# A new order for the fill of a chunked recurrence, and one scaling moved from VectorE to GpSimd

## The reference

```python
def step(S, inp):
    r_t, w_t, k_t, v_t, a_t, b_t = inp
    sa = jnp.einsum('bhij,bhj->bhi', S, a_t)
    S = (S * w_t[:, :, None, :] + sa[..., None] * b_t[:, :, None, :]
         + v_t[..., None] * k_t[:, :, None, :])
    return S, jnp.einsum('bhij,bhj->bhi', S, r_t)
_, y = lax.scan(step, S0, seq_in)   # over 528 positions
```

## Time and profile before

| | |
|---|---|
| median of 3 runs | 1512.23 us (1511.02 to 1512.6) |
| time of the profiled execution | 1514.68 us |
| its span in the profile | 1513.0 us |
| TensorE busy | 1436.7 us, 95% of the span |
| VectorE busy | 1033.1 us, 68% |
| ScalarE busy | 739.6 us, 49% |
| GpSimd busy | 93.5 us, 6% |
| chunk stage | from 878.15 us to about 1069 us of the span |

### The profile page before, as it was taken

The page is one execution under the profiler, slowest core; times in us unless marked ns, Lnnn a source line. Parts: engine busy times, 40 slices in busy tenths (PEclk is TensorE's granted clock), DMA queues, the critical chain, the costliest instruction groups (busy, mean ns, idle before and its releaser), DMA issues.

```text
span 1513.0 us, 30344 instructions
## 1 busy us (share of the span) xinstructions
PE 1436.7 (95%) x12931; PEld 1322.3 (87%) x12931; DVE 1033.1 (68%) x1463; ACT 739.6 (49%) x1071; POOL 93.5 (6%) x120
## 2 busy tenths in 40 slices
PE   6999999999999999998999967999799999999997
PEld 5898898999999999998999756889467898899986
DVE  5667577588844787577868665776678884488732
ACT  4555465445532455457588532433454553255422
POOL 3010011000030000000000231110000000000010
PEclk9999999999999999999999977999999999999999
DMA  4212221423433333555222232332333343334331
GB/s 126 67 57 63 64 70 50 113 84 98 123 92 100 92 92 88 158 162 173 83 74 77 70 85 47 60 57 40 113 84 98 98 123 104 95 85 112 86 96 56
DMA packets 283990, 136.78 MB, mean 90 GB/s; under 512 B 65449, under 2 KB 278593, under 8 KB 283601
## 3 DMA queue, kind: packets, MB, share of 16 engines
q1 hardware_dynamic: 283552, 134.77, 32.4%
q10 hardware_dynamic: 304, 0.08, 0.0%
HBM read 124.33 MB, written 10.49 MB: 89 GB/s over the span
## 4 chain that ended last, share of the span: by engine, by line
PE 74%; DVE 11%; ACT 6%; issue 3%; DMA 3%; POOL 1%; SPq 0%; DVEq 0%; POOLq 0%; ACTq 0%
PE psg L1882 25%; PE psx L1723 13%; PE psg L1723 11%; PE psg L2688 6%; PE psg L590 2%; DVE w_lo L136 2%; PE psx L590 2%; PE psg L618 2%; PE psg L674 1%; ACT rest_hi L330 1%; PE psx L3334 1%; DVE rest_lo L429 1%; DVE sum_lo L446 1%; ACT rest L316 1%; ACT w_hi L132 1%
## 5 line engine op out<-in xcount | busy, mean ns | idle before, releaser
L132 ACT ACTIVATE w_hi<-w_raw 128x1024 fp32r<-128x1024 f32 (+1 forms) x122 | 141.9, 1164 | 209.8 <-PE psg L1882 148.1
L1882 PE MATMUL psg<-mid_hi_l,w_hi 128*128 128x264 f32 (+1 forms) x720 | 232.8, 323 | 2.3 <-DVE w_lo L136 1.3
L1882 PE MATMUL psg<-mid_lo_l,w_hi 128*128 128x264 f32 (+1 forms) x720 | 231.6, 322 | 0.0
L1882 PE MATMUL psg<-mid_hi_l,w_lo 128*128 128x264 f32 (+1 forms) x720 | 231.0, 321 | 0.0
L136 DVE TENSOR_TENSOR w_lo<-w_raw,w_hi 128x1024 fp32r<-128x1024 f32 (+1 forms) x121 | 165.0, 1365 | 77.5 <-ACT w_hi L132 77.0
L1882 PEld LDWEIGHTS psg<-mid_hi_l,w_hi 128*128 128x128 f32 x720 | 135.3, 188 | 14.1 <-DVE w_lo L136 2.0
L1882 PEld LDWEIGHTS psg<-mid_lo_l,w_hi 128*128 128x128 f32 x720 | 135.3, 188 | 10.5 <-issue 0.2
L1882 PEld LDWEIGHTS psg<-mid_hi_l,w_lo 128*128 128x128 f32 x720 | 135.4, 188 | 10.3
L2688 PE MATMUL psg<-x_hi,w_hi 128*128 128x264 f32 (+1 forms) x320 | 99.7, 312 | 7.9 <-DVE w_lo L136 7.9
L2688 PE MATMUL psg<-x_lo,w_hi 128*128 128x264 f32 (+1 forms) x320 | 98.8, 309 | 0.0
L2688 PE MATMUL psg<-x_hi,w_lo 128*128 128x264 f32 (+1 forms) x320 | 98.7, 309 | 0.0
(11 more groups left out here) (518 smaller groups left out, 4336.1 us busy)
## 6 DMA issues: line engine op xcount, KB each, us to landing
w_raw<-in_w_ffn_out_dram SPq DMA_DIRECT2D x40, 704.0 KB, 4.7
w_raw<-in_w_qkv_dram SPq DMA_DIRECT2D x24, 512.0 KB, 3.7
w_raw<-in_w_rkv_dram SPq DMA_DIRECT2D x24, 512.0 KB, 3.9
x_raw_l<-in_w_ffn_in_dram SPq DMA_DIRECT2D x18, 512.0 KB, 4.1
x_raw_l<-in_w_ffn_in_dram SPq DMA_DIRECT2D x36, 256.0 KB, 4.7
w_raw<-in_w_ffn_in_dram SPq DMA_DIRECT2D x16, 512.0 KB, 3.8
y_raw_l<-in_w_ffn_in_dram SPq DMA_DIRECT2D x16, 512.0 KB, 4.0
y_raw_l<-in_w_ffn_in_dram SPq DMA_DIRECT2D x32, 256.0 KB, 4.5
```

Of the source, the lines that this page charges most:

```text
L132: k.nc.scalar.activation(k.w_hi[j][:, 0:kt, :], k.raw[j][:, 0:kt, :], ACT.Copy).then_inc(k.hi_ready[j].h, 1)
L1882: done = k.nc.tensor.matmul(self.bank(i, c), w[:, t, :], x, start=t == 0 and n == 0, stop=t == count - 1 and n == 2)
```

## The change

Five things change in `chunk_stage`.

1. The fill is written out as a list of its own on each engine, and the loop of steps starts at 0. TensorE turns and multiplies chunk 0 (`turn_bk`, `turn_v`, `quads`, `a_v`) before `l_products(2)`; VectorE does the two `keys` of chunk 0 before `small_blocks(0)`; in step 0 the gate, a filler and the state come earlier than before.
2. `turn_v` writes the lower 64 partitions instead of the upper, and calls `transpose` instead of a product with the identity. To match, the two planes of `bk` and the two halves of `uv` and `akm` change places.
3. `low_kept` becomes two buffers.
4. SyncE's order becomes, for each n, `keep_inverse(n)`, `fetch_inverse(n)`, then `keep_low(n+1)`, `fetch_lanes(n+1)`. In the fill `keep_low(0)`, `keep_low(1)` and their lanes go first.
5. The scaling of `rr` moves from VectorE's `products` to GpSimd's, as its third operation, ahead of the signal `scaled_p`.

```diff
             def keep_low(n):
                 sp.wait_ge(low_r.h, n + 1)
-                if n:
-                    sp.wait_ge(lane_in.h, 16 * n)
+                if n >= 2:
+                    sp.wait_ge(lane_in.h, 16 * (n - 1))
                 for half in range(2):
-                    sp.dma_start(by_heads(k.low_kept, half), low[n % 3][half_rows(half), :, :]).then_inc(low_out.h, 16)
+                    sp.dma_start(by_heads(k.low_kept[n % 2], half), low[n % 3][half_rows(half), :, :]).then_inc(low_out.h, 16)
...
-            for c in range(-3, CHUNKS - 2):
-                if c + 3 < CHUNKS:
-                    keep_low(c + 3)
-                    fetch_lanes(c + 3)
-                if c == -3:
...
-                else:
-                    keep_inverse(c + 2)
-                    fetch_inverse(c + 2)
+            fetch_lanes(0)
+            keep_low(1)
+            fetch_lanes(1)
...
+            for n in range(CHUNKS):
+                keep_inverse(n)
+                fetch_inverse(n)
+                if 1 <= n < CHUNKS - 1:
+                    keep_low(n + 1)
+                    fetch_lanes(n + 1)
...
         def gpsimd(pool):
...
-                nc.gpsimd.tensor_tensor(bk[n % 3][:, :, 0, :], chunk(r.aa, n), ch.w_inv[:], ALU.mult)
-                nc.gpsimd.tensor_tensor(chunk(r.kk_in, n), chunk(r.kk_in, n), ch.w_inv[:], ALU.mult).then_inc(scaled_p.h, 1)
...
+                nc.gpsimd.tensor_tensor(bk[n % 3][:, :, 1, :], chunk(r.aa, n), ch.w_inv[:], ALU.mult)
+                nc.gpsimd.tensor_tensor(chunk(r.kk_in, n), chunk(r.kk_in, n), ch.w_inv[:], ALU.mult)
+                nc.gpsimd.tensor_tensor(chunk(r.rr, n), chunk(r.rr, n), ch.w_ext[:, :, 1:C + 1], ALU.mult).then_inc(scaled_p.h, 1)
...
         def vector(dve):
             def products(n):
                 dve.wait_ge(exps.h, n + 1)
-                nc.vector.tensor_tensor(chunk(r.xn, n), chunk(r.xn, n), ch.w_ext[:, :, 0:C], ALU.mult)
-                nc.vector.tensor_tensor(chunk(r.rr, n), chunk(r.rr, n), ch.w_ext[:, :, 1:C + 1], ALU.mult)\
+                nc.vector.tensor_tensor(chunk(r.xn, n), chunk(r.xn, n), ch.w_ext[:, :, 0:C], ALU.mult)\
                     .then_inc(scaled_v.h, 1)
...
             products(1)
-            dve.wait_ge(scaled_v.h, 2)
+            keys(0, 0)
+            keys(0, 1)
+            small_blocks(0)
+            last_blocks(0)
+            products(2)
+            small_blocks(1)
+            last_blocks(1)
+            products(3)
+            small_blocks(2)
             steps(dve, step)
...
                 pe.wait_ge(bkt_r.h, n + 1)
                 settle()
                 for m in range(KT):
-                    last = mm(pair_ps[C:P, m // 4, (m % 4) * P:(m % 4) * P + P], r.vv[:, m, n * C:n * C + C], k.ident[:],
-                              start=True, stop=True)
+                    last = nc.tensor.transpose(pair_ps[0:C, m // 4, (m % 4) * P:(m % 4) * P + P],
+                                               r.vv[:, m, n * C:n * C + C], k.ident[:])
                 last.then_inc(tv_d.h, 1)
...
             pe.wait_ge(k.pads.h, 16)
             front_evicted(pe)
+            l_products(0)
+            turn_bk(0)
+            keep(8)
+            l_products(1)
+            turn_v(0)
+            keep(8)
+            quads(0, 0)
+            keep(8)
+            quads(0, 1)
+            keep(8)
+            a_v(0, 0)
+            keep(32)
+            l_products(2)
+            keep(24)
             steps(pe, step)
```

More of the change, by code:

```diff
@@ L2967, in steps @@
         def steps(eng, step):
-            for c in range(-3, CHUNKS):
-                step(c, c + 1, c % 2, 0 <= c, 0 <= c + 1 < CHUNKS)
+            for c in range(CHUNKS):
+                step(c, c + 1, c % 2, c + 1 < CHUNKS)
         res_in, g_in, g_split, gate_d, gate_r = (
@@ L3046, in decays, with lower @@
                 if n > 1:
-                    nc.scalar.activation(bk[(n - 1) % 3][:, :, 1, :], chunk(r.kk_in, n - 1), ACT.Copy).then_inc(bk_r.h, 1)
+                    nc.scalar.activation(bk[(n - 1) % 3][:, :, 0, :], chunk(r.kk_in, n - 1), ACT.Copy).then_inc(bk_r.h, 1)
                 nc.scalar.activation(ch.w_ext[:, :, 1:C + 1], chunk(r.gs, n), ACT.Exp, scale=DECAY)
                 nc.scalar.activation(ch.w_inv[:], chunk(r.gs, n), ACT.Exp, scale=-DECAY).then_inc(exps.h, 1)
-            def step(c, n, q, chain, prep):
+            def lower(n):
+                act.wait_ge(lps.h, n + 1)
+                nc.scalar.activation(low[n % 3][:], l_ps, ACT.Copy).then_inc(low_r.h, 1)
@@ L3052, in step @@
+            def step(c, n, q, prep):
                 p = 1 - q
-                if c + 3 < CHUNKS:
-                    act.wait_ge(lps.h, c + 4)
-                    nc.scalar.activation(low[c % 3][:], l_ps, ACT.Copy).then_inc(low_r.h, 1)
+                if c + 3 < CHUNKS and c:
+                    lower(c + 3)
                 if prep:
-                    act.wait_ge(tb_d.h, n + 1)
-                    nc.scalar.activation(bkt[p][:].rearrange("p m a c -> p (m a) c"),
-                                         pair_ps.rearrange("p b (m c) -> p (b m) c", c=C),
-                                         ACT.Copy).then_inc(bkt_r.h, 1)
@@ L3237, in reads, with grow, step @@
                                         quad_ps[:, :, :, 0:C], masks(ch.incl[:]), ALU.mult).then_inc(arm_r.h, 1)
-            def step(c, n, q, chain, prep):
-                p = 1 - q
-                if c == 0:
+            def grow(q, c):
+                dve.wait_ge(s_d.h, c + 1)
+                nc.vector.tensor_tensor(ch.state[:], ch.state[:], s_ps, ALU.add).then_inc(s_step.h, 1)
+                dve.wait_ge(s_step.h, c + 1)
+                dve.wait_ge(wend_r.h, c + 1)
+                nc.vector.tensor_tensor(ch.state[:], ch.state[:], w_end[q][:].broadcast_to([P, KT, C]),
+                                        ALU.mult).then_inc(state_r.h, 1)
+            def step(c, n, q, prep):
+                p = 1 - q
+                dve.wait_ge(av_r.h, c + 1)
+                if c:
+                    dve.wait_ge(w_d.h, c)
+                    nc.vector.scalar_tensor_tensor(wt[:], wy_ps, -1.0, av[q][:], ALU.mult, ALU.subtract)\
+                        .then_inc(wt_r.h, 1)
+                else:
+                    nc.vector.tensor_scalar(wt[:], av[q][:], -1.0, None, ALU.mult).then_inc(wt_r.h, 1)
                     dve.wait_ge(g_split.h, 1)
@@ L3308, in l_products @@
                 for h, m, rows in heads:
-                    last = mm(l_ps[rows, m, :], r.xn[rows, m, n * C:n * C + C], bk[n % 3][rows, m, 0, :],
+                    last = mm(l_ps[rows, m, :], r.xn[rows, m, n * C:n * C + C], bk[n % 3][rows, m, 1, :],
                               start=True, stop=True)
@@ L3357, in a_v @@
                 for h, m, rows in heads:
-                    last = mm(a_ps[rows, m, :], akm[C:P, at(h), :], uv[p][C:P, at(h), :], start=True, stop=True)
+                    last = mm(a_ps[rows, m, :], akm[0:C, at(h), :], uv[p][0:C, at(h), :], start=True, stop=True)
                 last.then_inc(av_d.h, 1)
@@ L3420, in chain_u @@
                 for h, m, rows in heads:
-                    last = mm(u_ps[0:C, h % 2, m * C:m * C + C], xt[q][rows, m, :], wt[rows, m, :], start=True,
+                    last = mm(u_ps[C:P, h % 2, m * C:m * C + C], xt[q][rows, m, :], wt[rows, m, :], start=True,
                               stop=True)
@@ L3450, in gate, with step @@
                    skip_group_check=True).then_inc(gate_d.h, 1)
-            def step(c, n, q, chain, prep):
+            def step(c, n, q, prep):
                 p = 1 - q
-                if c + 3 < CHUNKS:
-                    l_products(c + 3)
-                if c < -1:
-                    keep(24)
-                if prep:
+                if c == 0:
                     turn_bk(n)
-                if c == 0:
                     turn_v(n)
                     chain_u(c, q)
+                    l_products(3)
                     chain_s(c, q)
                     quads(n, 0)
+                    gate(c)
+                    keep(8)
                     times_x(n, p, 0)
```

185 lines of the change are left out of this document (97 added, 88 removed).

## The result

The changed kernel takes 1539.32 us in the median of 4 runs (1538.33 to 1540.32), the kernel before beside it 1512.41 (1511.02 to 1513.68). The ratio is 1.0178 with a 95% interval of 1.0160 to 1.0196: slower by 27 us. The forecast was 1537, within 1521 to 1550. Of all the series in this document two executions ran in a slower state of the chip (1585.48 and 2010.18 us), and medians and ranges are of the others. The profiled execution took 1540.1 (the working of the forecast ended at 1539.8), its span is 1538.4.

What follows compares the result with a forecast made beforehand. The steps were taken as bound by TensorE with a small VectorE share. The loop's 25.9 us less 0.85 for turning gave 25.1 more: 1514.68 became 1539.8, less 2.45 to the median 1537, range 1521 to 1550.

Steps and rivals of the forecast that it cites:

- the closed loop: Chunk stage: SyncE's new order makes small_blocks(n+1) wait for a full round of transfers; TensorE waits some 5 us a step.
- A turn of the loop: From one last_blocks to the next through SyncE's transfers, small_blocks and wt: 21.2 us (19.1 to 23.0) against 17.94, six times.
- The fill: Start of the chunk stage, until chain_u(0): 924.0 against 922.87, costing 1.1 us instead of saving any.
- The first round: In the fill, behind last_blocks(1), through keep_low(2): 16.7 us, so small_blocks(2) ends at 923.4.
- Step 0 at the low clock: Step 0's products run slower after TensorE's idle time of some 18 us, taken as 3 us: last_blocks(2) ends at 938.3.
- The end: State of step 6 comes 1.1 us behind the six turns, at 1066.6 against 1040.65: 25.9 later; the rest goes along.
- The turning: turn_v as 8 rows takes about 1.04 us instead of 1.89, saving 0.85 in step 7 alone.
- The scaling: rr scaled by GpSimd: one wait ahead of l_products replaces another at the same moment, 0 us, hidden in the loop.
- The bound without the cover: Scaling of rr by GpSimd, if TensorE's loop waits didn't hide it: up to 0.7 us in each of five steps.
- the rule weighed in the prediction: VectorE instructions with two SBUF inputs and GpSimd ones reading SBUF can't run at once; about 3 us more without the loop.
- The clock rival: TensorE's clock falls in every step after its waits: about 1555 us, 1573 if throughout; chance 0.12.

Runs made afterwards that it cites:

- The filler experiment: 8 filler products in TensorE's wait ahead of l_products, steps 1 to 5, added to the changed kernel with SyncE's old order: 1506.13 us, ratio 0.9961.

## Why the prediction was right, step by step

**The mechanism.** It is the closed loop: shown by the chain, by undoing the order (33 us less), by doing the order of the six turns alone (21 us more), and by making the loop shorter and longer with the time following. The number came out closer than its terms: what follows has misses of 1 to 3 us in both directions, and that they nearly cancel is luck.

**A turn of the loop: 21.2 predicted, 21.22 measured.** The sum is better than its terms. In the turn shown, `keep_inverse` to `fetch_inverse` took 4.83 (predicted 3.8, within its 3.3 to 5.0), the four fetches 3.76 because one issue took 1.66 (predicted 2.9), `keep_low` to `fetch_lanes` 3.31 (predicted 4.6), the lanes 2.69, `small_blocks` 2.6, `wt` and the rest as predicted. The 4.6 was a wrong choice between 3.3 and 4.7. I took the row that followed four fetches directly, as if the fetches had slowed the landing; the cause wasn't the neighbourhood, since six of seven such spacings after are 3.28 to 3.44. What made up for it was the longer landings and issues: landings of 4.27, 4.18, 4.12 and 4.01 are on the chain. On average of the six turns the four terms measured 3.8, 3.5, 3.5 and 3.3 where 3.8, 2.9, 4.6 and 2.7 were predicted: 14.0 either way, with one term 1.1 too long and two 0.6 too short. A single turn ranged from 20.26 to 22.16.

**The fill.** `small_blocks(0)` began at 890.68 (predicted 890.4), `last_blocks(0)` ended at 896.94 (896.6). `last_blocks(1)` ended at 909.66 instead of 906.7. The term that was missing are three small instructions, held by GpSimd's three scalings of chunk 3. The rows of both engines:

```profile
900.76 1.00 DVE L3211 TENSOR_SCALAR lane_x<-lane_low 64x8 f32<-64x8 f32 x1 [2.81 <-DMA inverse_turned_kept<-lane_xt]
901.80 1.20 DVE L3215 TENSOR_SCALAR lane_x<-lane_low 64x8 f32<-64x8 f32 x1
902.92 0.15 DVE L3216 TENSOR_TENSOR lane_sums<-lane_low,lane_x 64x8 f32<-64x8 f32 x1
903.10 1.04 DVE L3217 SCALAR_TENSOR_TENSOR lane_x<-lane_low,lane_sums 64x8 f32<-64x8 f32 x1
```

```profile
900.44 1.29 POOL L3142 TENSOR_TENSOR bk<-rows,w_inv 128x512 f32<-128x512 f32 x1 [10.40 <-ACT w_inv L3052]
901.69 1.28 POOL L3143 TENSOR_TENSOR rows<-rows,w_inv 128x512 f32<-128x512 f32 x1
902.93 1.19 POOL L3144 TENSOR_TENSOR rows<-rows,w_ext 128x512 f32<-128x512 f32 x1
```

The three slow rows end at 901.76, 903.00 and 904.14, the three of GpSimd at 901.73, 902.97 and 904.12. In the kernel with VectorE scaling (new order) GpSimd has two operations there and two rows are slow. So the third operation cost about 1 us in the fill of the changed kernel, which the prediction had at 0, and the other two 1.9 that it hadn't seen either. The first round was then shorter (3.3 for the triangle), so `chain_u(0)` came at 925.21, 1.2 late.

**Step 0 at the low clock.** `last_blocks(2)` was predicted to end at 938.3 and ended at 939.00, 13.8 behind `chain_u(0)` where 14.3 was predicted; 11.3 was the sum at the full clock, so the clock cost about 2.5 and not 3. Behind the wait of 19.78 us `chain_s` took 1.97 instead of 1.15:

```profile
925.21 1.65 PE L3462 MATMUL psx<-wt,xt 64*64 64x64 f32 x26 [19.78 <-DVE wt L3288]
...
928.82 1.97 PE L3481 MATMUL psx<-uv,bkt 128*64 128x64 f32 x32
```

**The end.** `last_blocks(8)` ended at 1066.34 (predicted 1065.5). The state of step 6 was predicted at 1066.6 and came at 1068.85, 28.2 later than in the kernel before instead of 25.9. I had it follow VectorE; it followed TensorE, whose `chain_s` took 1.90 at the low clock:

```profile
1066.90 1.90 PE psx L3481 x32
1068.80 2.01 PE psx L3388 x16
```

At the load of `res` the delay was 28.0 (1090.09 against 1062.13), where 25.1 was predicted, and that wait and the next gave 1.26 back (10.31 and 3.90 against 11.21 and 4.26). The span is 25.4 longer: 2.9 too much in the stage and 2.6 less behind it, of which 1.3 weren't traced. That the sum hit 25.1 is luck.

**The turning.** 8 rows take 1.06 (predicted 1.04). The step of it ahead of a covered `wt` is hidden, as predicted. The 0.85 that was to show from step 6 to step 7 isn't to be seen: from `state` to `state` it took 15.48 where it had taken 15.64, since the granted clock was at its low level for part of it (0.50 in 1064 to 1068, 0.64 in 1068 to 1072).

**The scaling.** In the steps of the changed kernel it is on no chain, as predicted; the times leave 0 to 4.6 us open, and the fill had about 1 of it. The bound without the cover was 0.7 a step, 3.5 us; measured are 4.6. The bound covered the longer wait (0.38 a step), but neither the 1.4 us in the fill nor the lower clock behind that wait. The third operation was taken as 1.27 alone; with VectorE's turn in it, it took 1.62.

That it is a matter of turns was said by the rule weighed in the prediction, of the Trainium skill's "SBUF — State Buffer", section "Who interferes with whom": the trace agrees with it (GpSimd's third operation 1.63 instead of 1.17 to 1.19, VectorE's 1.11 instead of 0.68), and its 3 us without the loop were near my upper bound of 3.5 and not near my 0; 4.6 were measured. The prediction said that no row decided it. One did, and wasn't read: in the kernel before VectorE's first scaling in the step of the earlier trace rows took 1.01 and not 0.68, beside GpSimd's second operation:

```profile
977.47 1.01 DVE L3132 TENSOR_TENSOR rows<-rows,w_ext 128x512 f32<-128x512 f32 x1
978.39 0.68 DVE L3133 TENSOR_TENSOR rows<-rows,w_ext 128x512 f32<-128x512 f32 x1
```

GpSimd's ended at 977.92, VectorE's at 978.48, 0.56 later. A second stood in the rows themselves: the first small instruction of the fill took 1.00 and of the step 0.16. It ended at 889.34, GpSimd's operation beside it at 889.30.

**The clock rival.** It was there in small (0.85 on average over the turns, as said above). In the stretch of step 1 (columns as above):

```profile
960.00:964.00 4.00, 4.00 (x78) 3.85 (x75) 2.43 (x6) 0.00 (x0) 0.00 (x0) 0.50 0.27 33
964.00:968.00 4.00, 4.00 (x104) 3.55 (x104) 1.86 (x4) 0.98 (x2) 0.00 (x0) 0.87 0.37 81
968.00:972.00 4.00, 2.67 (x66) 2.04 (x59) 3.03 (x5) 1.19 (x2) 4.00 (x3) 1.00 0.60 124
```

It fell to the 1.2 GHz level and was back by 968. Most of it went into the wait for `wt`, as the prediction had it; what wasn't hidden was the drop in step 0 and the last one, in front of the state of step 6.

## What to carry to other kernels

Before moving an instruction in an in-order DMA queue, write down what it waits for and who waits for it, and see whether the two ends meet: a round trip that was free beside others becomes the length of a step once its order closes a loop, and then every landing and every issue in it counts in full (one call moved within the loop gave 19 us back here). And an operation moved to an idle engine is free only as long as something else is the bound and the two engines don't hold each other up: look in the trace before for rows longer than their like beside that engine, and test with the cover taken away. When two traces are compared, count from the start of the stage: here it began up to 6.8 us apart in executions of kernels that are the same up to there.

## What the runs showed of the hardware that was not expected

- VectorE and GpSimd took turns, also where VectorE's instruction has one small input: 64x8 elements, 0.16 to 0.17 us as a rule, lasted 0.81 to 1.20 and ended within 0.03 us of GpSimd's scaling of a 128x512 tile in all six rows shown here (five have one input, one has two). A VectorE row that fell where one operation of GpSimd ended and the next began wasn't longer (0.15 at 902.92).
- An issue of one DMA on SyncE's queue, 0.57 to 0.67 us as a rule, took 1.24 to 1.81 for one of the four fetches in six of the nine rounds of the changed kernel. Why wasn't found.
- Landings on the chain came mostly at 2.6 to 2.8 us, four at 4.0 to 4.3, and few between (3.09 and 3.56). A sum of one value for each term was right over six turns, and off by up to 1 us for one.
- A wait of TensorE of 1.54 us was followed by a lower granted clock (0.68 in the 4 us shown) in two of four steps, one of 1.16 in none of four. The filler experiment took the drops away without a gain in time, so what they cost by themselves stays open.
